# Half of a 1024 x 1024 output projection as three F32R products, and two weight loads issued later, in a one-core hybrid decoder layer

## The reference

```python
merged = (gts[..., 0, :] * y_conv + gts[..., 1, :] * y_swa
          + gts[..., 2, :] * y_ret + gts[..., 3, :] * y_nsa)      # 1024 x 1024
mix = merged @ w_out                                              # w_out 1024 x 1024
x1 = layer_norm(ALPHA * x + mix, ln1_g, ln1_b)
scores = sigmoid(x1 @ router_w.T)        # 64 scores, 6 chosen per token by groups
out = layer_norm(ALPHA * x1 + routed_experts(x1) + shared_expert(x1), ln2_g, ln2_b)
```

## Time and profile before

| | |
|---|---|
| median of three runs | 2090.15 us |
| all three | 2086.91, 2090.62, 2090.15 us |
| span of the profiled execution | 2086.9 us (the time of the run at 2086.91 us; nothing measurable lies around the span) |
| busy share PE, DVE, ACT, POOL | 97%, 64%, 41%, 26% |
| row projection L1615, busy | 114.4 us, of it 4.2 us of waiting ahead |
| stretch from the barrier to its end | 1019 to 1150 us |
| expert loop | about 1225 to 2010 us |

### The profile page before, as it was taken

One profiled execution on the slowest core, in us unless ns is written; L12 is line 12 of the kernel. 1 busy time (PEld: TensorE's weight loads), 2 busy tenths in 40 slices (PEclk: granted clock), 3 DMA queues, 4 the chain that ended last, 5 costly groups with the idle time before them and its releaser, 6 DMA issues.

```text
span 2086.9 us, 33128 instructions
## 1 busy us (share of the span) xinstructions
PE 2019.1 (97%) x9741; PEld 1433.4 (69%) x9742; DVE 1341.2 (64%) x2793; ACT 851.9 (41%) x1434; POOL 551.0 (26%) x358
## 2 busy tenths in 40 slices
PE   8999999999999999989999999999999999999995
PEld 7887787877778666668555556666667666667662
DVE  2894534444026777788456657777777777777756
ACT  2111221244112444430022256666666666666643
POOL 2342231323322210012100133322233333233324
PEclk9999999999999999999999999999999999999998
DMA  6122221212612210268550378899898989899857
GB/s 198 51 70 88 76 61 31 88 50 66 167 61 81 70 48 19 75 201 284 205 239 31 133 303 296 303 345 343 318 333 272 352 286 336 307 305 310 292 169 195
DMA packets 167745, 389.05 MB, mean 186 GB/s; under 512 B 26192, under 2 KB 98161, under 8 KB 142960
## 3 DMA queue, kind: packets, MB, share of 16 engines
q1 hardware_dynamic: 129696, 298.02, 39.2%
q0 software_dynamic: 28752, 73.18, 14.1%
q10 hardware_dynamic: 9216, 16.78, 2.1%
HBM read 337.04 MB, written 80.22 MB: 200 GB/s over the span
## 4 chain that ended last, share of the span: by engine, by line
PE 35%; DMA 9%; issue 3%; DVE 2%; ACT 1%; ACTq 1%; DVEq 0%; POOLq 0%
DMA work<-x1d,idx 9%; PE e_bank L1690 8%; PE e_bank L1675 7%; PE e_bank L1615 5%; PE e_bank L1653 3%; PE e_bank L1623 3%; PE e_bank L1671 2%; PE e_bank L1672 2%; PE e_bank L1673 2%; ACT d_hi L1959 1%; PE e_bank L1643 1%; PE e_bank L1724 1%; PE e_bank L1761 1%; PE e_bank L1824 0%; PE e_bank L1702 0%
## 5 line engine op out<-in xcount | busy, mean ns | idle before, releaser
L646 PE MATMUL a_bank<-x_hi,w_hi 128*128 128x512 f32 x928 | 373.0, 402 | 0.0
L646 PE MATMUL a_bank<-x_hi,w_lo 128*128 128x512 f32 x928 | 362.5, 391 | 0.0
L646 PE MATMUL a_bank<-x_lo,w_hi 128*128 128x512 f32 x928 | 361.6, 390 | 0.0
L1675 PE MATMUL e_bank<-w_gu,work 128*128 x616 | 277.1, 593 | 2.2 <-issue 1.4
L2190 DVE TENSOR_TENSOR d_lo<-w_d,d_hi 128x1024 fp32r<-128x1024 f32 x152 | 179.8, 1224 | 58.7 <-ACT d_hi L1959 58.7
L581 POOL CAST w_hi<-w_raw 128x1024 fp32r<-128x1024 f32 x56 | 64.7, 1156 | 560.6 <-PE a_bank L646 560.6
L646 PEld LDWEIGHTS a_bank<-x_hi,w_hi 128*128 128x128 f32 x928 | 174.3, 188 | 40.8 <-issue 6.1
L646 PEld LDWEIGHTS a_bank<-x_hi,w_lo 128*128 128x128 f32 x928 | 174.1, 188 | 37.8
L646 PEld LDWEIGHTS a_bank<-x_lo,w_hi 128*128 128x128 f32 x928 | 174.6, 188 | 33.8 <-issue 0.5
L1675 PEld LDWEIGHTS e_bank<-w_gu,work 128*128 128x128 f32 x616 | 111.8, 191 | 113.4 <-issue 113.4
L1871 ACT ACTIVATE u_hi<-w_gu 128x1024 fp32r x150 | 159.0, 1061 | 2.0 <-POOL work L1564 1.7
(11 more groups left out here) (368 smaller groups left out, 3795.7 us busy)
## 6 DMA issues: line engine op xcount, KB each, us to landing
w_d<-in_moe_wd SPq DMA_DIRECT2D x64, 1024.0 KB, 12.9
w_gu<-in_moe_wg SPq DMA_DIRECT2D x64, 1024.0 KB, 7.9
w_gu<-in_moe_wu SPq DMA_DIRECT2D x64, 1024.0 KB, 11.5
w_raw<-in_w_in SPq DMA_DIRECT2D x53, 512.0 KB, 3.9
gates<-gate_out ACTq DMA_DIRECT2D x64, 256.0 KB, 2.0
g_sb<-gates SPq DMA_DIRECT2D x16, 1024.0 KB, 6.1
acc_odd<-zero POOLq DMA_DIRECT2D x9, 512.0 KB, 14.6
work<-in_w_out SPq DMA_DIRECT2D x4, 1024.0 KB, 9.3
```

The source lines that it names most:

```text
L646: ins = pe.matmul(bank[h][:, :], w[:, c % 2, k, :], x[:, k, cols], start=(k == 0 and j == 0), stop=(k == KD - 1 and j == 2))
L1675: ins = pe.matmul(out, x_gt[:, s, k, :], w_gu[:, bass.ds(e & 3, 1), :, k, :].rearrange('p a m f -> p (a m) f'), start=k == 0, stop=k == KD ...
```

## The change

In each tile of the row projection, the blocks k = 0 to 3 stay F32 matmuls, for both halves first. The blocks k = 4 to 7 become 24 F32R matmuls, three products for each k and half.

For this ScalarE copies `w_out`'s blocks 4 to 7 into `wo_hi` (four operations, at the address of the first two slots of `w_d`), and VectorE subtracts them in place into `wo_lo`. Per tile, ScalarE makes `m_hi` (128x512, two buffers in the place of the last turned x1) and GpSimd subtracts in place into `m_lo`. TensorE waits before its ninth matmul: in tile 0 for all of `wo_lo`, in every tile for `m_lo`. The first two m_hi and m_lo are made before tile 0; m_hi of tile t + 2 is made behind the square root of tile t, and the m_lo of tiles 2 to 7 behind GpSimd's zero-fill issues.

`wo_hi` lies where the down weights of experts 0 and 1 were loaded, so these two loads move behind `load_up(1, 1)`, after the last x1 store.

```diff
+        wo_hi = nc.alloc_sbuf_tensor_at('wo_hi', [P, 4, D], F32R, offset=rings_at + 4 * 2 * KD * S)
+        wo_lo = nc.alloc_sbuf_tensor_at('wo_lo', [P, 4, D], F32R, offset=rings_at + 4 * 4 * D)
+        m_hi = nc.alloc_sbuf_tensor_at('m_hi', [P, 2, 4, P], F32R, offset=late_at + 4 * (NT - NU - 1) * D)
+        m_lo = nc.alloc_sbuf_tensor_at('m_lo', [P, 4, S], F32R, offset=work_at + 4 * 4 * S)
...
@@ sync
-            load_down(0, 0)
-            load_down(1, 1)
             for t in range(NT):
                 if t == NT - 1:
                     sp.wait_ge(mix_done, NT)
...
             load_up(1, 1)
+            load_down(0, 0)
+            load_down(1, 1)
             for t in range(NU, NT):
@@ gpsimd
+            def merged_low(t):
+                pool.wait_ge(m_hi_ready, t + 1)
+                cols = slice(t * P, (t + 1) * P)
+                pool.tensor_tensor(m_lo[:, :, cols], merged[:, 4:8, cols], m_hi[:, t % 2, :, :].bitcast(F32), ALU.subtract
+                                   ).then_inc(m_lo_ready, 1)
             pool.memset(zero, 0.0).then_inc(zero_set, 1)
             pool.wait_ge(zero_set, 1)
+            for t in range(2):
+                merged_low(t)
             pool.wait_ge(mix_done, 1)
...
+            for t in range(2, NT):
+                merged_low(t)
@@ tensor, rows_out
-                for h in range(2):
-                    for k in range(KD):
-                        ins = pe.matmul(bank[2 * (t % 2) + h][:, :], merged[:, k, t * P:(t + 1) * P],
-                                        w_out[:, k, h * HALF:(h + 1) * HALF], start=k == 0, stop=k == KD - 1)
+                    for k in range(4):
+                        pe.matmul(bank[2 * (t % 2) + h][:, :], merged[:, k, rows], w_out[:, k, h * HALF:(h + 1) * HALF],
+                                  start=k == 0, stop=False)
+                if t == 0:
+                    pe.wait_ge(wo_lo_ready, 4)
+                pe.wait_ge(m_lo_ready, t + 1)
+                for h in range(2):
+                    cols = slice(h * HALF, (h + 1) * HALF)
+                    for k in range(4):
+                        for i, (m, w) in enumerate(((m_hi[:, t % 2, k, :], wo_hi), (m_hi[:, t % 2, k, :], wo_lo),
+                                                    (m_lo[:, k, rows], wo_hi))):
+                            ins = pe.matmul(bank[2 * (t % 2) + h][:, :], m, w[:, k, cols], start=False,
+                                            stop=k == 3 and i == 2)
                 ins.then_inc(mix_done, 1)
@@ scalar
+            def merged_high(t):
+                if t >= 2:
+                    act.wait_ge(mix_done, t - 1)
+                act.activation(m_hi[:, t % 2, :, :], merged[:, 4:8, t * P:(t + 1) * P], ACT.Copy).then_inc(m_hi_ready, 1)
+            act.wait_ge(half_merged, 2 * KD)
+            act.wait_ge(wo_in, 64)
+            merged_high(0)
+            for k in range(4):
+                act.activation(wo_hi[:, k, :], w_out[:, 4 + k, :], ACT.Copy).then_inc(wo_hi_ready, 1)
+            merged_high(1)
             act.wait_ge(r_tr, 1)
...
                 act.activation(sd[:, t % 2:t % 2 + 1], mv[:, t % 2, 1:2], ACT.Sqrt, bias=eps[:, 0:1]).then_inc(sd_done, 1)
+                if t + 2 < NT:
+                    merged_high(t + 2)
@@ vector
             dve.wait_ge(half_merged, 2 * KD)
+            for k in range(4):
+                dve.wait_ge(wo_hi_ready, k + 1)
+                dve.tensor_tensor(wo_lo[:, k, :], w_out[:, 4 + k, :], wo_hi[:, k, :].bitcast(F32), ALU.subtract
+                                  ).then_inc(wo_lo_ready, 1)
             dve.wait_ge(ln_in, 32)
```

More of the change, by code:

```diff
@@ L1305, in back @@
         assert nc.sbuf_base == sh_at + 4 * 6144
+        late_at = (nc.sbuf_base + 31) // 32 * 32
         x1_late = sb('x1_late', [P, NT - NU, KD, P])
+        assert nc.sbuf_base == late_at + 4 * (NT - NU) * D
         turned_x1 = lambda t: x1_t[:, t, :, :] if t < NU else x1_late[:, t - NU, :, :]
@@ L1371, in back @@
         scored, tail_in = sem('scored'), sem('tail_in')
+        wo_hi_ready, wo_lo_ready, m_hi_ready, m_lo_ready = (
+            sem(n) for n in ('wo_hi_ready', 'wo_lo_ready', 'm_hi_ready', 'm_lo_ready'))
         d_hi_ready, d_lo_ready, h_hi_ready = sem('d_hi_ready'), sem('d_lo_ready'), sem('h_hi_ready')
@@ L1612, in rows_out @@
                     pe.wait_ge(pre_read, t - 1)
+                rows = slice(t * P, (t + 1) * P)
                 for h in range(2):
-                    for k in range(KD):
-                        ins = pe.matmul(bank[2 * (t % 2) + h][:, :], merged[:, k, t * P:(t + 1) * P],
-                                        w_out[:, k, h * HALF:(h + 1) * HALF], start=k == 0, stop=k == KD - 1)
+                    for k in range(4):
[11 more added lines that the diff above has]
+                                            stop=k == 3 and i == 2)
                 ins.then_inc(mix_done, 1)
```

## The result

The changed kernel takes 2078.61 us (median of four runs, 2077.22 to 2079.85) where the kernel before, run beside it, takes 2088.68 us (2086.91 to 2090.62). The ratio is 0.9947, its 95% interval 0.9936 to 0.9959: faster by 0.53%. The forecast was 2080.0 us with 2074.5 to 2085.5 as its range. The profiled execution fell from a span of 2086.9 us to 2075.4 us, 11.5 us, while the medians lie 10.1 us apart.

What follows compares the result with a forecast made beforehand. TensorE's length of work alone was taken to bound 1020 to 1150 us. Eight tiles' 10.3 us less 0.1 for the last tile gave 10.2 off the 2090.15 us median: 2080.0 us, range 2074.5 to 2085.5.

Steps and rivals of the forecast that it cites:

- Price of a triple: Row projection: 24 F32R matmuls cost 5.58 us a tile against 6.87 for the passes replaced, saving 1.29 us.
- Tile 0's parts: Tile 0: wo_lo ready at 1027.6 us, needed at 1030.05, 2.4 us spare, so costed at nothing; worst a 2.5 us wait.
- Rival (a): Tile 0: wo_lo comes late and the clock may fall, halving the gain to 4.7 us, 2085.5 us; chance 0.07.
- Tile 0's clock: Start of tile 0: slow passes until 1026.6 us are all ones that stay; the replaced part runs at full clock.
- VectorE: Steady tiles: shorter period and GpSimd overlap take 2.5 us of 3.9 spare, regained in the wait for the root.
- (b): Steady tiles: VectorE becomes the bound; at d = 3.9 us the time is 2087.5, no measurable change; chance 0.06.
- (c): Same place, larger price: at d of 5.0 us or more, 4 us slower, 2094; chance 0.02.
- d: Steady tiles: microseconds a tile that the GpSimd overlap costs VectorE; six tiles' gain shrinks from d = 2.6 on.
- Last tile: Last tile: the root doesn't wait for ScalarE's tables, so some VectorE lateness shows: 0.1 us, at most 1.0.
- The third tile: Shared weights land some 1.3 us earlier or more; VectorE's lateness grows 2.6 us once, into the waits for the root.
- Moved loads: Two 1 MB down loads issued behind load_up(1, 1) land by 1182 us, in time: cost nothing, bounds 0 and 1 us.
- Rival (e): Expert loop: gather waits answer to the new phase, 2.7 us either way; chance 0.02 of over 6 us taken.

Runs made afterwards that it cites:

- The run without cover: The changed kernel with tile 0's F32R triples ahead of its F32 passes, so nothing covers the making of wo_lo: 2083.48 us, ratio 0.9971.
- three operations: The changed kernel with three more VectorE maxima over the row of 1024, results unused, behind the root in every normed1: 2092.92 us, ratio 1.0014.

## Why the prediction was right

**What bounds the kernel.** TensorE's length alone set the time from 1020 to 1150 us. The series shows it best: 0, 2, 4 and 5 blocks replaced give periods of 16.79, 16.13, 15.46 and 15.13 us, 0.33 us a block throughout. Nothing else became the bound.

**Price of a triple.** 24 x 0.2292 + 0.08 = 5.58 us was forecast from the branch projections' row, and 5.53 was measured, 0.2304 us each. 1.33 us a tile instead of 1.29, 10.6 us instead of 10.3. Choosing spacing over duration decided this: the new matmuls' duration is 0.39 us like that of the earlier trace rows, and 24 x 0.39 = 9.4 against the 6.87 that the passes cost would have forecast a loss. Durations on both sides would have forecast next to no gain, since a pass shows 0.606 us and 16 x 0.606 = 9.7.

**Tile 0's parts.** wo_lo at 1027.6, needed at 1030.05; measured 1027.96 and 1030.65. The margin, 2.4 against 2.7, was right. GpSimd's overlap, which I had put only into the worst case, took 1.2 us of VectorE's time there; it was covered by hand-overs that cost nothing and by ScalarE, which began 1.4 us ahead of TensorE's first matmul and not with it. Rival (a) did not occur. The run without cover comes nearest to it, with wo_lo late and slow triples behind the wait, and costs 6.3 us; it is another case, since TensorE had done nothing ahead of the wait there, and the passes behind it got the full clock in exchange. What a wait of 2.5 us in the middle of tile 0 would cost was not run.

**Tile 0's clock.** This is the step that failed, in a small way. I took the slow phase as untouched, since the same passes stand in it. It was not constant: its excess over full clock is 3.22 us before and 2.75 and 2.90 after, 3.03 with the loads alone, and 1.93 with m_lo on VectorE, with two blocks and with five. It gave the profiled execution some 0.5 us that I didn't have; with 1.9 to 3.2 over the nine profiles that start tile 0 with F32 passes it follows none of the edits, and it is no dependable term. What differs is when the clock fell. Busy times in the microsecond ahead of TensorE's first matmul, the granted clock third from the end, first the changed kernel, then the one with five blocks:

```profile
1020.50:1021.50 1.00, 0.00 (x0) 0.00 (x0) 0.00 (x0) 1.00 (x2) 0.92 (x2) 0.50 0.26 62
1021.20:1022.20 1.00, 0.00 (x0) 0.00 (x0) 0.00 (x0) 1.00 (x3) 0.90 (x2) 1.00 0.23 52
```

In the three profiles with an excess of 1.93 us the clock was still 1.00 then and fell within the first 0.6 us of the work; in the six with 2.75 to 3.22 it had already fallen before TensorE began. TensorE's idle time was the same, 4.2 to 4.3 us, in all nine. What sets that moment no run here was made to show.

**VectorE.** Spare time 3.9 us, minus 1.33 for the period, minus up to 1.2 for the lock; it lost 0.94. The wait for the root was to fall to 1.7 to 3 us and is 2.1 to 2.3 in the last steady tiles. In the third tile it is 0.36, nothing that can be spent, and 1.21 in the fourth: the lateness from the shared weights' wait, which the prediction had, ate it there, and TensorE didn't wait. The lock is real, as the earlier trace rows had it, and no cost of it on the path shows in the run with m_lo on VectorE. By the Trainium skill (SBUF — State Buffer, Who interferes with whom), a VectorE instruction with two SBUF inputs contends with a GpSimd instruction that reads SBUF. The trace agrees, with 2.17 us against 1.23, while the reduction, with one input, took its own 1.22 beside GpSimd. Rivals (b) and (c) had the mechanism: with three operations d is 3.75 us and no lock besides, so each tile was to lose 3.75 - 2.6 = 1.15 us, and the period rose by 0.87. Their price for the whole was too low: six tiles at 1.15 are 6.9 us, and that run lost 13.5 us in the stage, 4.6 of them in the last tile's tail, which neither rival had; its added operations also stand in the last two tiles, where the rivals' overlap does not.

**Last tile.** 0.1 us, at most 1.0, was charged. From the end of the last row projection to the first expert block is 65.05 us after and 65.14 before. The lateness is not seen.

**The third tile.** The shared weights' transfer was to land "1.3 us earlier, or more, as the two down loads no longer share the queues". VectorE's operation behind it starts 27.4 us after tile 0's last matmul, against 27.9 before and 27.7 with the loads moved alone. So the earlier issue, which follows tile 0's end, holds, and the "or more" is 0.5 us, of which the moved loads show 0.2. VectorE's wait for it stayed, at 6.5 us against 6.6.

**Moved loads.** Costed at nothing; the run with the loads alone gives 1.0002 (0.9993 to 1.0011). The two loads are issued from 1149.15 us and the first acc store follows at 1163.76. The slowest of the kernel's down loads landed 18.9 us after its issue, against 22.2 in the earlier trace rows.

**Sum.** 10.2 us was forecast for the stage and 11.1 measured: 0.3 more from the triples, 0.1 from the last tile, 0.5 from tile 0's clock. The remaining 0.4 of the profiled 11.5 us is the front and the loop. The time came out 1.4 us below the forecast of 2080.0 although the medians fell by 10.1 us, nearly the forecast 10.2 (the ratio's 0.53% is 11.1 us, like the stage): the forecast started from 2090.15, the median of three runs, and the four runs beside the changed kernel have 2088.68. That the medians agree with 10.2 more closely than the stage does is luck, since they carry the scatter of the parts outside it.

**The loop.** Rival (e) was a widening, and rightly. Its gather waits are 21.7 us, in 29 turns, against 27.2 in the earlier trace rows. Over the ten profiles they run from 21.2 to 31.7 us and the part behind the stage from 869.2 to 874.0 us, the shortest with the shortest waits and the longest with the longest. The five runs of the changed kernel lie 3.5 us apart (2077.5 to 2081.0), the ten with two blocks 8.7 and the twenty of the kernel before 9.2. The part ahead of the stage moves by 4.7 us and the part behind it by 4.8 over the ten profiles, so the two together can make that up. What sets the gathers' waits in an execution no run here was made to show.

## What to carry to other kernels

Cost a matmul in a stream by the spacing of its neighbours' starts in the same pattern, not by its duration: it gave the new piece within 1%, where its duration set against the passes' spacing would have given the wrong sign. When work is moved to an engine off the path, add the spare time of that engine over one period, take from it what the shorter period itself removes and what contention takes, and see what remains; here 1.7 us of 3.9 in a steady tile, enough; look apart at a tile that is late for another reason and at the last, which has no next period to give the time back. And put what is already ready ahead of what must still be made: the same matmuls in the other order cost 6 us here.

## What the runs showed of the hardware

- The contention of the two engines works both ways and depends on the operation. VectorE's step with two SBUF inputs, L2086, went from 1.23 to 2.17 us and ended 1.08 us after GpSimd's piece. GpSimd's piece began in the last 0.44 us of the scaling step ahead, L2085, and took 1.57 us instead of 1.27, while L2085 kept its 0.81. Beside a reduction, 1.22 us, GpSimd took its 1.27.
- After 4.2 to 4.3 us of idle time TensorE's granted clock was 0.50 until 5.1 to 6.0 us into the work in six profiles, and until 3.8 to 3.9 us into it in three, where it was still 1.00 at the start of the work; after 10.9 us of waiting it was 0.50 for the first 4.4 us of the work. A piece behind TensorE's waits in the routing took 6.06 us instead of 3.49, with a granted clock of 0.59 over most of it, and 5.24 to 6.58 us over the ten profiles.
- Taking two transfers of 1 MB away from behind another let that one land at most 0.2 us earlier.
- The same code ahead of the stage takes 1019.2 to 1023.8 us from profile to profile, and the code behind it 869.2 to 874.0 us.
